# Four weight blocks of the expert stages loaded in pieces of 32, 45, 49 and 2 partitions, two of them late in the stage

## The chip, the cores and the metric

One Trainium2 chip, one core of it. The time is that of one execution on the device, in microseconds (us), the median of the runs shown. The core has five engines with a queue of instructions each: PE (matmul), DVE (vector), ACT (scalar), POOL (GpSimd) and SP (which here only issues DMAs). 16 DMA engines move the data for it.

## What is computed

Two transformer blocks on 256 tokens of 1024 features, one after the other, all in float32. The first block has two layers. Each layer ends in an expert stage (`peer_ffn`): for each token, 8 heads score two sets of 128 keys and choose 16 experts each out of 16384; of every chosen expert one row `u` and one row `v` of 1024 features are read:

```
q = (ht @ w_query).reshape(T, Hh, 2, PEER_HALF)
scores = einsum('thpd,hpkd->thpk', q, sub_keys)
...
u = expert_u[idx]
a = gelu(einsum('tkd,td->tk', u, xb)) * g
return einsum('tk,tkd->td', a, expert_v[idx])
```

So each layer reads 256 x 128 expert rows of 8 KB (u and v together), 256 MB (of 1024 x 1024 bytes). After layer 0's expert stage comes a gated MLP (`sgu`, whose first weight column is `("sgu_v", 6)`); after layer 1's comes the second block, whose mixer starts with the weight column `("w_in", 2)`.

## The kernel before

**Blocks.** Every weight matrix is stored in blocks of 128 partitions x 2048 float32 (1 MB, one row of 8 KB per partition). `blocks` lists them in the order of use. SP loads block i into the buffer `raws[raw_at[i]]` (4 in `ring`, and 2 early ones for each layer's query matrix). Before it is used, a block is split in two: ACT writes the rounded high part to `ring_high` (`highs`, line 2071), DVE the rest in place to `ring_low` (`lows`, line 1241). PE then multiplies in three products (lines 648 and 696).

**The expert stage** (`peer` on each engine). Tokens are on the partitions, 128 at a time, so one layer has 2 x 128 = 256 steps `s`. Step s is one gather by POOL (`gathers`, line 551): row `p_idx[:, s]` of `peer_uv` for each of the 128 partitions, 128 rows of 8 KB, 1 MB. It goes to one of 8 slots (`uv`, 6 in the arena, `uv_high`, 2 in `ring_high`; one of them opens at s = 40, `OPEN_AT`). Then DVE takes the dot product with u (line 1655, semaphore `dot_ready`), ACT makes gelu x gate and a diagonal matrix from it (lines 2258, 2262, 2266), and PE multiplies that matrix with v and adds up in PSUM (line 973, semaphore `uv_used`, which frees the slot: POOL's next gather into it waits for that).

Between the steps stands other work, at fixed s: PE computes the last query columns and scores up to s = 36 (`between`); DVE chooses the experts of the next heads (`choose`); the query blocks and the first blocks of the next matrix are split. At s = 40 POOL first waits for the last scores (line 919), since the slot that opens lies over tiles that they are computed from.

**The order around the change.** SP's queue is one loop over the blocks. For block i it waits until the block that was in the buffer has been used (`wait_block_free`), then issues one DMA. In layer 0 the blocks `first+4` to `first+7` (`first` is the first query block) are followed by `first+8` and `first+9`, the two blocks of `("sgu_v", 6)`; the block after them waits until all 256 dots are done (`behind_rows`). In layer 1 the query blocks are followed by eight blocks of `mem_kv`, and then by the two of `("w_in", 2)`. In both layers the blocks in question are first multiplied at s = 216 and 224 (`TILE_AT`). In layer 0 they are split together, by ACT at s = 40 and DVE at s = 42:

```
sp.dma_start(raws[raw_at[i]], blocks[i]).then_inc(w_in[raw_at[i]], 16)      # SP, line 512
highs(first + 9)        # ACT, s == 40
lows(first + 9)         # DVE, s == 42
```

In layer 1 the same calls split the first two `mem_kv` blocks; the two `w_in` blocks are split there by ACT at s = 154 and 170 and by DVE at s = 157 and 173. ACT waits for `16 * raw_count[i]` on the buffer's semaphore before it splits a block; `raw_count` counts the DMAs into that buffer so far.

## Time and profile before

| | us |
|---|---|
| median of 3 runs | 2271.21 (2267.56 to 2271.28) |
| the profiled execution | 2266.26 |
| its span, first to last instruction | 2264.5 |
| PE, DVE, ACT, POOL busy | 1979.4, 1561.4, 1023.1, 619.8 |

The profiled execution spends 1.8 us outside its span. In the profile, "DMA share" is the mean busy share of the 16 DMA engines (records overlap by a per cent, so that 1.01 is all of them busy), "GB/s" what they moved, and "idle" the time that an engine stood still before an instruction, with the one that ended it. "PEclk" is the TensorE clock granted, as a share of full speed; it is 0.98 over the span. The first expert stage runs from about 278 to 943 us, the second from about 1200 to 1882 us.

### The profile page before, as it was taken

What the parts mean: (1) busy time and instruction counts of PE and PEld (TensorE: products, weight loads), DVE (VectorE), ACT (ScalarE), POOL (GpSimd) and SP (SyncE); (2) the same over time, 40 slices, a digit from 0 to 9 for tenths busy, and PEclk for the clock granted to TensorE, in tenths of its full rate; (3) what the DMA queues carried; (4) which work ended last, traced back from release to release, by engine and by line L of the source; (5) the groups of instructions that cost most, each with busy time, mean ns of one, the idle gap of its engine ahead of it and who ended that gap; (6) DMA issues with size and microseconds to landing.
All of it is one profiled execution on the core that took longest, in us unless ns stands there. A gap on an engine that the chain in (4) does not pass through costs nothing. (4 is left out here: it accounts for less than half of the span.)

```text
span 2264.5 us, 23976 instructions
## 1 busy us (share of the span) xinstructions
PE 1979.4 (87%) x8056; PEld 1237.2 (55%) x8056; DVE 1561.4 (69%) x2947; ACT 1023.1 (45%) x2157; POOL 619.8 (27%) x559
## 2 busy tenths in 40 slices
PE   5999899778777888899989988888888879899998
PEld 4986766223222333379866534334333326878987
DVE  6977787766667776578877777667777755565654
ACT  4344345444444444445444554344464434544443
POOL 0000044543434434100003544443444440310000
PEclk9999999999999999999999999999999999999999
DMA  8886699999999999886669999999999995333553
GB/s 325 295 335 204 247 403 402 417 421 421 421 421 421 422 421 421 337 326 241 220 248 369 407 421 421 420 422 421 421 410 422 421 421 211 118 134 135 179 193 132
DMA packets 112396, 761.24 MB, mean 336 GB/s; under 512 B 12832, under 2 KB 13600, under 8 KB 26128
## 3 DMA queue, kind: packets, MB, share of 16 engines
q0 software_dynamic: 76480, 548.94, 58.6%
q1 hardware_dynamic: 34832, 207.74, 24.8%
q10 hardware_dynamic: 960, 3.01, 0.4%
q8 instruction: 64, 1.05, 0.2%
q14 instruction: 60, 0.49, 0.1%
HBM read 758.60 MB, written 1.05 MB: 335 GB/s over the span
## 5 line engine op out<-in xcount | busy, mean ns | idle before, releaser
L973 PE MATMUL pair<-uv,p_diag 128*128 128x512 f32 x1536 | 755.1, 626 | 175.0 <-ACT p_diag L2266 171.7
L1655 DVE CUSTOM_DVE_ANT_0 uv<-uv,p_h 128x1024 f32<-128x1024 f32 x384 | 469.8, 1224 | 300.7 <-DMA uv<-in_peer_uv,p_idx 299.4
L551 POOL DMA_INDIRECT uv<-in_peer_uv,p_idx x384 | 433.8, 1130 | 684.6 <-PE pair L973 552.7
L973 PEld LDWEIGHTS pair<-uv,p_diag 128*128 128x128 f32 x1536 | 277.4, 194 | 618.3 <-ACT p_diag L2266 363.3
L1241 DVE TENSOR_TENSOR ring_low<-ring,ring_high 128x2048 fp32r<-128x2048 f32 x144 | 328.9, 2297 | 115.4 <-ACT ring_high L2071 114.2
L2258 ACT ACTIVATE p_act<-p_dot 128x1 f32<-128x1 f32 x512 | 103.4, 202 | 625.4 <-DVE p_dot L1655 623.5
L2071 ACT ACTIVATE ring_high<-ring 128x2048 fp32r<-128x2048 f32 x144 | 271.5, 1908 | 176.6 <-DMA ring<-in_ret_w_in 49.5
L696 PE MATMUL pair<-hT_high,ring_high 128*128 128x256 f32 x960 | 286.4, 298 | 1.3 <-ACT b_cgT L2158 1.2
L973 PE MATMUL pair<-uv_high,p_diag 128*128 128x512 f32 x512 | 248.3, 617 | 36.1 <-ACT p_diag L2266 36.1
L696 PE MATMUL pair<-hT_low,ring_high 128*128 128x256 f32 x960 | 271.8, 283 | 0.0
L696 PE MATMUL pair<-hT_high,ring_low 128*128 128x256 f32 x896 | 253.8, 283 | 0.0
L2266 ACT ACTIVATE p_diag<-ident,p_w 128x128 f32<-128x128 f32 x512 | 205.6, 402 | 17.2
L1655 DVE CUSTOM_DVE_ANT_0 uv_high<-uv_high,p_h 128x1024 f32<-128x1024 f32 x128 | 156.6, 1223 | 80.9 <-DMA uv_high<-in_peer_uv,p_idx 79.4
L973 PEld LDWEIGHTS pair<-uv_high,p_diag 128*128 128x128 f32 x512 | 93.3, 194 | 182.1 <-ACT p_diag L2266 94.8
L696 PEld LDWEIGHTS pair<-hT_high,ring_high 128*128 128x128 f32 x960 | 184.4, 192 | 11.3 <-issue 9.6
L696 PEld LDWEIGHTS pair<-hT_low,ring_high 128*128 128x128 f32 x960 | 184.4, 192 | 7.8 <-issue 7.7
L551 POOL DMA_INDIRECT uv_high<-in_peer_uv,p_idx x128 | 144.9, 1132 | 141.5 <-PE pair L973 108.2
L2262 ACT ACTIVATE p_w<-p_act,p_gate 128x1 f32<-128x1 f32 x512 | 150.7, 294 | 49.2 <-ACT p_act L2258 0.8
L696 PEld LDWEIGHTS pair<-hT_high,ring_low 128*128 128x128 f32 x896 | 172.0, 192 | 0.0
L648 PE MATMUL pair<-ring_high,hT_high 128*128 128x512 f32 x240 | 97.7, 407 | 5.2 <-DVE ring_low L1241 3.7
L648 PE MATMUL pair<-ring_high,hT_low 128*128 128x512 f32 x240 | 94.1, 392 | 0.0
L648 PE MATMUL pair<-ring_low,hT_high 128*128 128x512 f32 x240 | 94.1, 392 | 0.0
(395 smaller groups left out, 2432.8 us busy)
## 6 DMA issues: line engine op xcount, KB each, us to landing
ada<-in_ada_w SPq DMA_DIRECT2D x50, 512.0 KB, 5.7
ring<-in_ret_w_in SPq DMA_DIRECT2D x24, 1024.0 KB, 6.4
ring<-in_sgu_w_in SPq DMA_DIRECT2D x24, 1024.0 KB, 6.2
ring<-in_w_up SPq DMA_DIRECT2D x16, 1024.0 KB, 4.8
ring<-in_w_down SPq DMA_DIRECT2D x16, 1024.0 KB, 4.7
mod<-in_ada_w SPq DMA_DIRECT2D x30, 512.0 KB, 6.5
ring<-in_peer_w_query SPq DMA_DIRECT2D x12, 1024.0 KB, 7.8
ring<-in_sgu_w_out SPq DMA_DIRECT2D x12, 1024.0 KB, 6.2
```

Of the source, the lines that this page charges most:

```text
L551: nc.gpsimd.indirect_dma_start(uv_rows[SLOT[l][s]].rearrange("p a d -> p (a d)"), None, experts, bass.IndirectOffsetOnAxis(ap=p_idx[:, k:k ...
L648: mm = nc.tensor.matmul(acc[:, t, :], a, b[:, k, :], start=(first and k == 0 and j == 0), stop=(last and k == BK - 1 and j == 2))
L696: mm = nc.tensor.matmul(acc[:, nt // 2, nt % 2 * S:(nt % 2 + 1) * S], a[:, k, n_tile], b[:, kk, :], start=(kk == 0 and nt % 2 == 0 and j = ...
L973: mm = nc.tensor.matmul(acc[:, half, :], p_diag[:, n % DIAGS, :], v[:, half * 512:(half + 1) * 512], start=(k == 0), stop=(k == PICKS - 1))
L1241: did(V.tensor_tensor(raw_lows[raw_at[i]], raws[raw_at[i]], ring_high[:, high_at[i]].bitcast(F32), ALU.subtract), w_low, i + 1)
L1655: V.tensor_tensor_reduce(out=u, in0=u, in1=p_h[:, s // PICKS, :], scale=1.0, scalar=0.0, op0=ALU.mult, op1=ALU.add, accum_out=p_dot[:, n % ...
L2071: did(A.activation(ring_high[:, high_at[i]], raws[raw_at[i]], ACT.Copy), w_high, i + 1)
L2258: did(A.activation(p_act[:, d:d + 1], p_dot[:, d:d + 1], ACT.Gelu_apprx_tanh))
L2262: did(A.activation(p_w[:, d:d + 1], p_act[:, d:d + 1], ACT.Copy, scale=p_gate[:, s % PICKS:s % PICKS + 1]))
L2266: did(A.activation(p_diag[:, n % DIAGS, :], ident[:], ACT.Copy, scale=p_w[:, d:d + 1]), diag_ready, n + 1)
```

## The change

Four blocks, the two of `("sgu_v", 6)` and the two of `("w_in", 2)`, are each loaded by four DMAs in place of one: partitions 0 to 31, 32 to 76, 77 to 125 and 126 to 127, that is 32, 45, 49 and 2. The bytes are the same, and ACT waits for all four. The two blocks of layer 0 are also issued later: SP waits for dot 140 and dot 156 before them. They are split one at a time, by ACT at s = 150 and 166 and by DVE at s = 152 and 168. In layer 1 neither the issue nor the split is moved.

```
+LATE_LOAD = (140, 156)
+LATE_SPLIT = (150, 166)
+ROW_GROUPS = ((0, 32), (32, 77), (77, 126), (126, 128))
...
-    raw_count = [sum(raw_at[j] == raw_at[i] for j in range(i + 1)) for i in range(limit)]
+    uneven = [first_block_of[("sgu_v", 6)], first_block_of[("sgu_v", 6)] + 1, first_block_of[("w_in", 2)], first_block_of[("w_in", 2)] + 1]
+    loads_of = [ROW_GROUPS if i in uneven else ((0, P),) for i in range(limit)]
+    raw_count = [sum(len(loads_of[j]) for j in range(i + 1) if raw_at[j] == raw_at[i]) for i in range(limit)]
...
-                sp.dma_start(raws[raw_at[i]], blocks[i]).then_inc(w_in[raw_at[i]], 16)
+                if i in uneven[0:2]:
+                    sp.wait_ge(dot_ready, LATE_LOAD[uneven.index(i)])
+                for lo, hi in loads_of[i]:
+                    sp.dma_start(raws[raw_at[i]][lo:hi], blocks[i][lo:hi]).then_inc(w_in[raw_at[i]], 16)
...
-                        if s == 42:
+                        if l == 1 and s == 42:
                             lows(first + 9)
+                        if l == 0 and s - 2 in LATE_SPLIT:
+                            lows(first + 8 + LATE_SPLIT.index(s - 2))
...
-                            highs(first + 9)
+                            if l == 1:
+                                highs(first + 9)
+                        if l == 0 and s in LATE_SPLIT:
+                            highs(first + 8 + LATE_SPLIT.index(s))
```

SP's queue from the last query block to the first blocks after the stage of layer 0, with what each row waits for. Before:

```order
L512 DMA ring<-in_peer_w_query 128x2048 [waits sum_ready]
L512 DMA ring<-in_sgu_w_in 128x2048 [waits w_used]
L512 DMA ring<-in_sgu_w_in 128x2048 [waits sum_ready]
L512 DMA ring<-in_sgu_w_in 128x2048 [waits dot_ready,w_used]
L512 DMA ring<-in_sgu_w_in 128x2048 [waits sum_ready]
```

and now:

```order
L520 DMA ring<-in_peer_w_query 128x2048 [waits sum_ready]
L520 DMA ring<-in_sgu_w_in 32x2048 [waits dot_ready,w_used]
L520 DMA ring<-in_sgu_w_in 45x2048
L520 DMA ring<-in_sgu_w_in 49x2048
L520 DMA ring<-in_sgu_w_in 2x2048
L520 DMA ring<-in_sgu_w_in 32x2048 [waits dot_ready,sum_ready]
L520 DMA ring<-in_sgu_w_in 45x2048
L520 DMA ring<-in_sgu_w_in 49x2048
L520 DMA ring<-in_sgu_w_in 2x2048
L520 DMA ring<-in_sgu_w_in 128x2048 [waits dot_ready,w_used]
L520 DMA ring<-in_sgu_w_in 128x2048 [waits sum_ready]
```

Two DMAs have become eight, and both groups now also wait for `dot_ready`. The next block behind them waited for `dot_ready` already, so nothing else in SP's queue is held up.

DVE's queue around s = 42 of layer 0 (the rows with `p_dot` are the dot products; the row with x2 splits both blocks). Before:

```order
L1655 ISA uv_high_99,p_dot<-uv_high_99,p_h 128x1024
L1655 ISA p_dot 128x1
L1548 MAX_INDEX p_pos<-p_top,p_s 128x8 x2
L1241 TENSOR_TENSOR ring_low<-ring,ring_high 128x2048 x2
L1655 ISA uv_92,p_dot<-uv_92,p_h 128x1024
L1655 ISA p_dot 128x1
```

and now, first there and then at s = 152:

```order
L1663 ISA uv_high_99,p_dot<-uv_high_99,p_h 128x1024
L1663 ISA p_dot 128x1
L1556 MAX_INDEX p_pos<-p_top,p_s 128x8 x2
L1663 ISA uv_92,p_dot<-uv_92,p_h 128x1024
L1663 ISA p_dot 128x1
...
L1598 TENSOR_SCALAR p_ef<-p_i 128x16
L1600 TENSOR_TENSOR p_idx<-p_ef,p_i 128x16
L1249 TENSOR_TENSOR ring_low<-ring,ring_high 128x2048
L1663 ISA uv_high_98,p_dot<-uv_high_98,p_h 128x1024
```

One split stands now between two dots where two stood before, 110 steps later; the second follows 16 steps behind it.

## Rows read from the trace of the kernel before

**Rows 1.** The page, its head and the 40 slices of the span.
```profile
span 2264.5 us, 23976 instructions
...
DMA  8886699999999999886669999999999995333553
GB/s 325 295 335 204 247 403 402 417 421 421 421 421 421 422 421 421 337 326 241 220 248 369 407 421 421 420 422 421 421 410 422 421 421 211 118 134 135 179 193 132
```

**Rows 2.** The costliest groups, both expert stages: busy, mean ns, idle before, releaser.
```profile
L973 PE MATMUL pair<-uv,p_diag 128*128 128x512 f32 x1536 | 755.1, 626 | 175.0 <-ACT p_diag L2266 171.7
L1655 DVE CUSTOM_DVE_ANT_0 uv<-uv,p_h 128x1024 f32<-128x1024 f32 x384 | 469.8, 1224 | 300.7 <-DMA uv<-in_peer_uv,p_idx 299.4
L551 POOL DMA_INDIRECT uv<-in_peer_uv,p_idx x384 | 433.8, 1130 | 684.6 <-PE pair L973 552.7
```

**Rows 3.** Timeline of POOL at the end of stage 0: start, duration, idle before.
```profile
895.27 0.93 POOL L551 DMA_INDIRECT uv<-in_peer_uv,p_idx  x1 [1.54 <-PE pair L973]
...
925.06 0.93 POOL L551 DMA_INDIRECT uv<-in_peer_uv,p_idx  x1 [1.54 <-PE pair L973]
```

**Rows 4.** Stage 0's end by windows: length, engines' busy, PEclk, DMA share, GB/s.
```profile
core 0: us, PE busy (x) PEld busy (x) DVE busy (x) ACT busy (x) POOL busy (x), PEclk, DMA share, GB/s
...
925.00:932.00 7.00, 5.70 (x12) 2.03 (x12) 3.70 (x6) 2.27 (x9) 0.93 (x1) 1.00 1.01 421
932.00:933.00 1.00, 0.50 (x2) 0.25 (x2) 0.13 (x1) 0.67 (x2) 0.00 (x0) 1.00 0.79 328
933.00:934.00 1.00, 1.00 (x3) 0.43 (x3) 1.00 (x1) 0.00 (x0) 0.00 (x0) 1.00 0.45 188
934.00:936.00 2.00, 1.52 (x4) 0.49 (x3) 0.80 (x3) 0.90 (x3) 0.00 (x0) 1.00 0.12 49
936.00:938.00 2.00, 1.55 (x4) 0.49 (x3) 0.77 (x3) 0.90 (x3) 0.00 (x0) 1.00 0.14 57
938.00:940.00 2.00, 1.64 (x4) 0.38 (x2) 1.01 (x2) 0.83 (x3) 0.00 (x0) 1.00 0.05 20
```

**Rows 5.** Timeline of DVE at stage 0's end: the last dots, the first exit step.
```profile
937.77 1.23 DVE L1655 CUSTOM_DVE_ANT_0 uv<-uv,p_h 128x1024 f32<-128x1024 f32 x1 [1.23 <-DMA uv<-in_peer_uv,p_idx]
...
940.23 1.23 DVE L1655 CUSTOM_DVE_ANT_0 uv<-uv,p_h 128x1024 f32<-128x1024 f32 x1 [1.22 <-DMA uv<-in_peer_uv,p_idx]
...
943.85 0.69 DVE L1755 TENSOR_TENSOR p_tmp<-pair,mod 128x512 f32<-128x512 f32 x1 [2.39 <-PE pair L973]
```

**Rows 6.** Stage 1's end by the same windows.
```profile
1873.00:1874.00 1.00, 0.67 (x2) 0.00 (x0) 0.07 (x2) 0.77 (x3) 0.00 (x0) 1.00 0.98 410
1874.00:1875.00 1.00, 0.82 (x2) 0.49 (x3) 0.67 (x1) 0.13 (x1) 0.00 (x0) 1.00 0.40 164
1875.00:1876.00 1.00, 1.00 (x3) 0.19 (x1) 0.57 (x2) 0.30 (x2) 0.00 (x0) 1.00 0.20 82
1876.00:1878.00 2.00, 1.49 (x4) 0.68 (x4) 1.21 (x2) 0.59 (x2) 0.00 (x0) 1.00 0.11 45
1878.00:1879.00 1.00, 0.66 (x2) 0.00 (x0) 0.02 (x2) 0.82 (x3) 0.00 (x0) 1.00 0.04 16
```

**Rows 7.** Timeline of SP's DMA queue: the layer 0 loads, the layer 1 loads; then `ring`'s own view, 280 to 420.
```profile
287.75 6.08 SPq L512 DMA_DIRECT2D ring<-in_sgu_w_in  x2
...
1541.80 356.87 SPq L512 DMA_DIRECT2D ring<-in_w_in  x6
...
L512 SPq DMA_DIRECT2D ring<-in_sgu_w_in x2: 327/328/328, 287.7 to 293.5; - x2
...
DMA to landing us min/median/max: 9.3/9.4/9.6
```

**Rows 8.** Stage 0's first half by windows.
```profile
281.00:303.00 22.00, 18.36 (x118) 14.91 (x118) 15.42 (x57) 8.98 (x16) 6.34 (x6) 0.92 1.01 422
303.00:313.00 10.00, 10.00 (x51) 6.70 (x50) 8.17 (x23) 7.28 (x17) 5.52 (x4) 1.00 1.01 420
313.00:331.00 18.00, 16.77 (x72) 10.14 (x71) 17.09 (x41) 9.93 (x25) 11.20 (x7) 1.00 0.97 381
331.00:357.00 26.00, 26.00 (x117) 16.43 (x117) 19.71 (x44) 15.44 (x38) 14.69 (x12) 1.00 1.00 411
357.00:389.00 32.00, 32.00 (x125) 18.60 (x125) 21.89 (x58) 13.71 (x42) 12.40 (x12) 1.00 1.01 419
389.00:394.00 5.00, 5.00 (x25) 3.09 (x24) 3.38 (x11) 4.24 (x10) 2.39 (x3) 1.00 0.75 286
```

**Rows 9.** Timeline of POOL at s = 40: the wait for the last scores.
```profile
391.00 0.57 POOL L538 DMA_DIRECT2D s_wsT<-in_ws_turned  x1 [6.03 <-PE small L919]
```

**Rows 10.** Timelines of ACT and DVE: the two blocks split at s = 40 and 42.
```profile
401.37 3.71 ACT L2071 ACTIVATE ring_high<-ring 128x2048 fp32r<-128x2048 f32 x2
...
406.61 4.47 DVE L1241 TENSOR_TENSOR ring_low<-ring,ring_high 128x2048 fp32r<-128x2048 f32 x2
```

**Rows 11.** The DMA queue's issues: KB each, us from issue to landing.
```profile
ring<-in_sgu_w_in SPq DMA_DIRECT2D x24, 1024.0 KB, 6.2
```

## The prediction

> **What bounds the kernel now.** I read the head of the page first. Over both expert stages the 16 DMA engines are busy and move 421 GB/s [rows 1]; together the stages are some 1350 of the 2264.5 us. The costliest groups say the same from the engines' side: each dot product waits for its gathered rows (299.4 us of idle time), ACT's and PE's idle time follows from that, and POOL waits for PE, which frees the slots [rows 2]. At the end of stage 0, 13 gathers are issued from 895.27 to 925.06, so one every 29.79 / 12 = 2.48 us [rows 3]. That is 1 MB at 421 GB/s. A weight block is also 1 MB [rows 11], so loading one inside the stage takes 2.49 us of all 16 engines. In rows: a gather or a block is 128 rows of 8 KB, 8 for each DMA engine, and a row takes one engine 2.49 / 8 = 0.311 us.
>
> Next I read how the stage ends, as that tells whether the 16 engines finish together. They don't. In stage 0 all are busy until 932; from 932 to 934 the share falls from 0.79 to 0.45, and from 934 to 938 it is 0.12 to 0.14, which is 2 of 16; then one is left, into the last us before 940 [rows 4]. All that time dots still start every 2.46 us and wait for a DMA, the last at 940.23 [rows 5]. So the pace at the end is that of two DMA engines that lag. I put the ordinary fourteen at 933.3 (the middle of their fall), the laggards at 938.2 and 939.8. The busy time left after 932 is 0.79 + 0.45 + 0.24 + 0.28 + 0.10 = 1.86 us of all 16: spread evenly, the work would end at 933.9, **6 us sooner**. Stage 1 has the same tail: ordinary ones near 1874.3, laggards at about 1877.6 and 1878.8 [rows 6]. The even end there would be 1873 + (0.98 + 0.40 + 0.20 + 0.22 + 0.04) = 1874.8, **4 us sooner**. These 10 us are the most that dealing the bytes out differently can bring.
>
> Last I read stage 0's first half, since two loads leave it. The blocks are issued at 287.75 and 293.5, while the DMA share is 1.01 [rows 7, 8]. But PE is as full there: 10.00 of 10, 16.77 of 18, 26.00 of 26 and 32.00 of 32 us from 303 to 389, and the next gate, POOL's wait for the last scores, ends at 391.00 by PE [rows 8, 9]. DMA and PE bind together until s = 40.
>
> **Part 1, the loads and splits of layer 0 move from the first gathers and s = 40 to s = 140 and 150.** Removed early: 2 x 2.49 = 5.0 us of DMA time. What the gate at 391 gains is between 0 (PE is full) and 5.0 (DMA alone binds); no row shows the stage with less to load. PE's only slack from 303 to 389 is 1.23 us [rows 8], so the value lies near the low end: I take 0.7. The laggards carry some of the early load past the gate, though: their lag is 6.3 us over 659 us of stage, in proportion 1.1 us by 394, where the share has fallen to 0.75 and so ordinary engines are already idle [rows 8]. I take 1.5 us that they catch up beside the 0.7 (ends 0 and 4.3).
> Added late: the same bytes, in a stretch where every engine is busy to the end, so here they cost in full. Dealt out evenly that is 5.0 us on each engine.
> The splits: 3.71 us of ACT and 4.47 us of DVE stood at s = 40 and 42 [rows 10]; now half of each comes at 150 and again at 166. Both are hidden by the gathers in flight: the last one was issued at 925.06 and used at 940.23, 15 us later [rows 3, 5], six gathers deep, so 2.3 us of delay starves no DMA engine. If that cover were gone, each split would cost up to 2.3 us. A load is issued some 25 us before its split, against 9.4 us from issue to landing of the two loads in question [rows 7]. SP issues six more DMAs per layer, on a queue with nothing else in it.
>
> **Part 2, the pieces.** No row shows how 45 or 49 partitions are dealt out, as all large loads here have 128. I assume whole equal shares over as many of the 16 as divide the count, from the first engine on: 32 = 16 x 2, 45 = 15 x 3, 49 = 7 x 7, 2 = 2 x 1. Then a block gives 13 rows to two engines, 12 to five, 5 to eight and 2 to the last one, where each had 8. For the two blocks of a stage, at 0.311 us a row, that is 8.1, 7.5, 3.1 and 1.2 us in place of 5.0. The ends are an even spread (nothing changes) and shares that put the load on the laggards (a loss). I assume the laggards among the lightly loaded nine, one with 2 rows and one with 5.
> What the rows alone show is that two engines lag. The Trainium skill names a pair: in "DMA: Bandwidth & Descriptors", under "Latency and other measured facts", engines 7 and 15 are usually slower where the descriptors come from software. Under "Why a DMA increments its semaphore by 16 and not by 1" the same page gives the deal assumed above, on the lowest-numbered engines; by it engine 7 gets 5 rows and engine 15 gets 2. By these two rules the sum is the one below.
>
> **The sum.** Stage 0, everything 0.7 sooner after the gate: the laggards end at 939.8 - 0.7 - 1.5 + 1.2 = 938.8 and 938.2 - 0.7 - 1.5 + 3.1 = 939.1, the heavily loaded at 933.3 - 0.7 + 8.1 = **940.7**. The last was at 939.8: +0.9 us. So the lag is filled up, but with work that was free before. Stage 1, where nothing moves and the loads come at 1541.80 and later, in the full stretch [rows 7]: the laggards 1878.8 - 3.7 = 1875.1 and 1877.6 - 1.9 = 1875.7, the heavily loaded 1874.3 + 3.1 = **1877.4**: -1.4 us. Together **-0.5 us**. The profiled execution would go from 2266.3 to 2265.8 us. It stood 4.9 us below the median of the runs, so for the median I say 2271.2 - 0.5 = **2270.7 us**.
>
> **The rivals.**
> *The early DMA time counts* (faster). If the first gathers and not PE set the time to s = 40, the gate gains some 4 us. For it: the share 1.01 from 281 to 313. Against it: PE at 10.00 of 10 and 32.00 of 32. Stage 0 then ends at 933.3 - 4 + 8.1 = 937.4 (-2.4), stage 1 brings -1.4 to, where the heavily loaded ones are the first of the fourteen to finish, -2.6: -3.8 to -5.0 us, about 2266.5.
> *The laggards are among the heavily loaded* (slower). The trace doesn't number its DMA engines. If a laggard gets 13 rows a block, stage 0 ends at 939.8 - 0.7 - 1.5 + 8.1 = 945.7 (+5.9) and stage 1 at 1878.8 + 3.1 = 1881.9 (+3.1): +9.0, 2280 us. It decides as soon as a laggard gets more than 8 rows. For it: the rows leave open which engines lag. Against it: both tails are alike, two laggards of nearly the same size, so the lag seems to belong to a fixed pair, and nine of the 16 are lightly loaded. I choose 0.10, below what a blind draw of the pair would give. What keeps it low is the pair that the Trainium skill names, above.
> *The pieces don't change the deal.* If every engine still gets 8 rows, only the move is left: 939.8 - 0.7 - 1.5 + 5.0 = 942.6, +2.8 us in stage 0 and 0 in stage 1, 2274.0. The trace can't exclude it.
> A rule speaks for this one. In its "Rules for kernel authors" the same page of the Trainium skill advises one transfer of 128 partitions over transfers to disjoint parts, since they serialize on the same engines: by that the pieces bring nothing and the sum is this rival's.
>
> **How the numbers follow.** What a measurement of this kernel can tell from no change is about 0.2%, 4.5 us. The forecast has a chance of 0.55, the first rival 0.25, the second 0.10, the third 0.10. The forecast lies within 4.5 us of no change with nearly all its weight: its own bounds are +3 (no gain at the gate, no catching up) and -3. The first rival I count as faster, though half of it lies at the bound; the second is slower, and of the third 0.03, as the runs scatter by 3.7 us. So faster 0.25, the same 0.62, slower 0.13. The range runs from 2264.0 (the first rival, with a us for the runs' scatter) to 2275.5 (the third rival, with a little more); it leaves out the second rival and the far end of the first.
>
> **What would show it.** In the windows at the end of the stages the tail should be short: the share falls in steps over the last 2 to 3 us, five to seven engines finish last rather than two, and there is no stretch of 4 us at 0.12. The last dot of stage 0 should start at about 941, in stage 1 about 1.4 us sooner counted from that stage's start. At the gate, POOL's wait should end within a us of 391, and the share between 389 and 394 should be lower than 0.75 or fall earlier. The layer 0 loads should be issued near 650 and 690. A tail that is longer than before, with one or two engines, would show the laggards were loaded; a tail as before in stage 1 shows the pieces are dealt evenly; a gate at 387 shows the first rival. The forecast is wrong if the time moves by over 4.5 us.

## The result, and the profile after

Before: 2271.24 us (median of 4 runs, 2267.56 to 2273.85). After: **2299.34 us** (4 runs, 2297.72 to 2302.56). The ratio is 1.014, with a 95% interval of 1.0126 to 1.0155: 1.4% slower. The medians are 28 us apart; 1.4% of 2268 us is 32 us (29 to 35). Forecast were 2270.7 and at most 2275.5 us. The execution that was profiled took 2302.56 us, with a span of 2300.8. It is the slowest of its four, and the profiled one of before (2266.26 us) is faster than the median, so the two traces lie 36 us apart, more than the medians.

The page of the kernel after, its head and the costliest groups, which answer to [rows 1, 2]:

```profile
span 2300.8 us, 23991 instructions
...
DMA  8886699999999999886669999999999996333453
GB/s 322 291 331 213 252 359 407 422 422 421 421 385 362 421 421 421 338 340 232 223 245 373 404 420 421 420 422 382 355 402 423 421 421 231 113 135 131 183 191 137
...
L981 PE MATMUL pair<-uv,p_diag 128*128 128x512 f32 x1536 | 769.1, 636 | 193.5 <-ACT p_diag L2276 190.6
L1663 DVE CUSTOM_DVE_ANT_0 uv<-uv,p_h 128x1024 f32<-128x1024 f32 x384 | 470.4, 1225 | 333.5 <-DMA uv<-in_peer_uv,p_idx 333.1
```

The dots are as long as before (1225 ns) and wait 33 us longer for their rows: 333.1 where 299.4 stood. The GB/s line has two holes that weren't there, 385 and 362 in stage 0, 382 and 355 in stage 1, while the DMA digits above them stay 9. The engines don't stand idle; they are busy and move less. The windows around the two loads of layer 0, and then of layer 1 (length, busy time and count of PE, PEld, DVE, ACT and POOL, PEclk, DMA share, GB/s), put the holes where the loads are:

```profile
640.00:651.00 11.00, 10.00 (x22) 3.89 (x21) 8.08 (x25) 4.04 (x14) 6.66 (x6) 0.97 1.01 422
651.00:667.00 16.00, 9.21 (x16) 2.90 (x14) 4.69 (x14) 2.69 (x9) 3.72 (x5) 0.82 1.01 288
667.00:701.00 34.00, 24.92 (x46) 9.53 (x47) 25.10 (x60) 16.16 (x43) 12.70 (x12) 0.85 1.02 423
701.00:718.00 17.00, 10.35 (x19) 3.61 (x17) 4.51 (x15) 2.69 (x9) 5.63 (x5) 0.87 1.01 282
718.00:724.00 6.00, 3.78 (x4) 1.17 (x4) 5.69 (x7) 0.90 (x3) 0.00 (x0) 0.60 1.02 423
724.00:736.00 12.00, 10.38 (x20) 4.47 (x20) 9.44 (x24) 8.05 (x21) 5.16 (x5) 0.78 0.87 328
```

```profile
1550.00:1562.00 12.00, 12.00 (x40) 7.26 (x39) 9.37 (x27) 5.55 (x14) 3.73 (x3) 1.00 1.02 422
1562.00:1578.00 16.00, 10.28 (x20) 3.85 (x19) 5.75 (x12) 2.80 (x10) 6.56 (x6) 0.89 1.02 281
1578.00:1612.00 34.00, 28.92 (x66) 13.88 (x67) 24.03 (x62) 14.84 (x43) 11.15 (x11) 0.85 1.01 420
1612.00:1630.00 18.00, 11.88 (x28) 4.72 (x26) 7.25 (x16) 4.92 (x13) 7.31 (x7) 1.00 1.02 283
```

Each load is followed by 16 to 18 us at 281 to 288 GB/s, at a DMA share of 1.01 or 1.02. What a window loses is its length times (1 - rate / 421): 5.1, 5.6, 5.3 and 5.9 us, 21.9 in all. After the second load of layer 0 there is a different loss. From 724 to 736 the share itself falls, to 0.87: no gather was issued in time, 12 x (1 - 328/421) = 2.7 us. Stage 1 has a like dip some 50 us after its second load, from 1660 to 1673; here are the dip, and the whole stretch from the first load to its end:

```profile
1660.00:1673.00 13.00, 12.74 (x35) 6.24 (x33) 10.76 (x28) 6.25 (x16) 6.42 (x5) 1.00 0.84 314
1560.00:1673.00 113.00, 90.06 (x202) 40.14 (x200) 68.82 (x168) 44.27 (x119) 42.83 (x38) 0.89 0.99 365
```

The whole stretch loses 113 x (1 - 365/421) = 15.0 us. Stage 1, counted from its first gather to its last dot, took 695.9 us where it had taken 680.7: the 15.2 are all there. Stage 0, counted in the same way, grew by 17.3 us, from 661.8 to 679.2.

How it reaches the other engines shows in DVE's timeline over the first load (start, duration, idle before and its releaser). Dots that came every 2.46 us [rows 5] come 6.8 and 7.7 us apart:

```profile
653.11 1.22 DVE L1663 CUSTOM_DVE_ANT_0 uv<-uv,p_h 128x1024 f32<-128x1024 f32 x1 [0.85 <-DMA uv<-in_peer_uv,p_idx]
...
659.88 1.23 DVE L1663 CUSTOM_DVE_ANT_0 uv<-uv,p_h 128x1024 f32<-128x1024 f32 x1 [5.00 <-DMA uv<-in_peer_uv,p_idx]
...
667.56 1.23 DVE L1663 CUSTOM_DVE_ANT_0 uv<-uv,p_h 128x1024 f32<-128x1024 f32 x1 [6.03 <-DMA uv<-in_peer_uv,p_idx]
```

And POOL, which issues the next gather into a slot that a finished row frees, then waits for PE, so the late rows come back a second time as late gathers:

```profile
657.71 0.94 POOL L559 DMA_INDIRECT uv<-in_peer_uv,p_idx  x1 [1.55 <-PE pair L981]
666.27 0.94 POOL L559 DMA_INDIRECT uv<-in_peer_uv,p_idx  x1 [7.63 <-PE pair L981]
674.23 0.94 POOL L559 DMA_INDIRECT uv<-in_peer_uv,p_idx  x1 [7.02 <-PE pair L981]
```

The single packets of the trace say what the engines do in those 16 us. A packet of 8 KB takes 314 ns elsewhere in the stage, nearly without scatter, whichever queue it is of. While the pieces of a block are in flight, for 13.5 to 14.8 us, 70 to 87% of the packets take 400 to 620 ns and 2 to 5% stay under 330, with a mean of 494 to 520 over the four blocks, **the gathers' packets no less than the load's**. The starts of the load's packets also fit the deal that the prediction assumed: two waves of 16, then 45 in waves that run into each other, then seven waves of 7, some 1 us apart, then 2. Which engine takes which row they don't show, as the trace doesn't number the engines.

The places that the prediction had named, in the order SP's timeline, the gate on POOL and the end of stage 0 (windows, then the last dot), for [rows 7, 9, 4, 5]:

```profile
649.46 51.39 SPq L520 DMA_DIRECT2D ring<-in_sgu_w_in  x8
```

```profile
279.59 1.03 POOL L559 DMA_INDIRECT uv<-in_peer_uv,p_idx  x1 [84.54 <-DVE p_idx L1628]
...
392.20 0.57 POOL L546 DMA_DIRECT2D s_wsT<-in_ws_turned  x1 [6.03 <-PE small L927]
```

```profile
303.00:313.00 10.00, 10.00 (x53) 6.93 (x52) 9.33 (x30) 6.76 (x17) 5.12 (x4) 1.00 0.79 270
...
389.00:394.00 5.00, 4.66 (x24) 2.78 (x22) 2.76 (x8) 4.61 (x10) 1.49 (x2) 1.00 0.90 371
...
951.00:953.00 2.00, 1.79 (x4) 0.68 (x4) 1.23 (x2) 0.43 (x3) 0.00 (x0) 1.00 0.48 201
953.00:957.00 4.00, 3.02 (x7) 1.17 (x7) 1.95 (x3) 1.52 (x5) 0.00 (x0) 1.00 0.14 57
957.00:958.00 1.00, 1.00 (x3) 0.19 (x1) 0.52 (x2) 0.35 (x2) 0.00 (x0) 1.00 0.10 41
```

```profile
958.74 1.23 DVE L1663 CUSTOM_DVE_ANT_0 uv<-uv,p_h 128x1024 f32<-128x1024 f32 x1 [1.22 <-DMA uv<-in_peer_uv,p_idx]
```

From the first gather to the gate it took 392.20 - 279.59 = 112.61 us; before it was 391.00 - 278.40 = 112.60. Nothing was gained there, though the DMA engines moved 270 GB/s from 303 to 313 in place of 420: PE was full then, as before. The share around the gate, forecast below the 0.75 of before, was 0.90. The tail at stage 0's end is as long as it was, two engines for 4 to 5 us; the five to seven engines that were to finish last aren't seen.

### The profile page after: what moved, and what is told of

Its sections match the earlier page's. It is cut to its first block and busy times, and to the rows that moved or that the text cites. A ratio compares the mean times of both kernels' runs of the same rounds, so it can differ in the third digit from the quotient of the medians.

```text
span 2300.8 us, 23991 instructions
## 1 busy us (share of the span) xinstructions
PE 1990.4 (87%) x8056; PEld 1243.0 (54%) x8056; DVE 1563.4 (68%) x2947; ACT 1022.9 (44%) x2157; POOL 616.8 (27%) x559
## 5 line engine op out<-in xcount | busy, mean ns | idle before, releaser
L981 PE MATMUL pair<-uv,p_diag 128*128 128x512 f32 x1536 | 769.1, 636 | 193.5 <-ACT p_diag L2276 190.6
L1663 DVE CUSTOM_DVE_ANT_0 uv<-uv,p_h 128x1024 f32<-128x1024 f32 x384 | 470.4, 1225 | 333.5 <-DMA uv<-in_peer_uv,p_idx 333.1
L981 PEld LDWEIGHTS pair<-uv,p_diag 128*128 128x128 f32 x1536 | 283.1, 198 | 646.0 <-ACT p_diag L2276 382.6
L559 POOL DMA_INDIRECT uv<-in_peer_uv,p_idx x384 | 427.1, 1112 | 719.2 <-PE pair L981 582.7
```

The source lines that it names most:

```text
L559: nc.gpsimd.indirect_dma_start(uv_rows[SLOT[l][s]].rearrange("p a d -> p (a d)"), None, experts, bass.IndirectOffsetOnAxis(ap=p_idx[:, k:k ...
L981: mm = nc.tensor.matmul(acc[:, half, :], p_diag[:, n % DIAGS, :], v[:, half * 512:(half + 1) * 512], start=(k == 0), stop=(k == PICKS - 1))
L1663: V.tensor_tensor_reduce(out=u, in0=u, in1=p_h[:, s // PICKS, :], scale=1.0, scalar=0.0, op0=ALU.mult, op1=ALU.add, accum_out=p_dot[:, n % ...
```

## The experiments

Each change to the time is the ratio less 1, times 2268 us, with its 95% interval; "before" was run beside each batch (medians 2267.9 to 2268.7, 13 to 21 runs a batch). "Only in layer 1" means that the two `w_in` blocks, loaded in the full stretch after 1541, are the only ones touched. All others load as before. Where a stage's own time is given, it is that of the one profiled execution, from the first gather to the last dot; stage 0 takes 660.6 to 662.2 us in the sixteen traces in which nothing in it was changed, so a difference of a us or so in it says nothing.

### Taking the change apart

**late_whole**: the move alone, `ROW_GROUPS` not used.

```diff
-    loads_of = [ROW_GROUPS if i in uneven else ((0, P),) for i in range(limit)]
+    loads_of = [((0, P),) for i in range(limit)]
```

> The changed kernel with its four blocks loaded whole again; only the move of layer 0's two loads and splits to s = 140 to 168 is left. After the change stage 0 (first gather issued to last dot) grew by 17.3 us and stage 1 by 15.3 us; at 651 to 667 and 701 to 718 us, right after the loads of pieces, the DMA share stayed 1.01 while 288 and 282 GB/s were moved in place of 421. Theory 1, the pieces slow all DMA while they are loaded, whenever that is: late_whole costs only the 5.0 us of DMA time that were free before, at most, +2 to +5 us against before, no window under 415 GB/s around the loads. Theory 2, a load that falls into the full stretch costs much more than its bytes: +15 to +20 us, and low GB/s at the same places.

**pieces_early**: the pieces in all four blocks, loads and splits at their old places (the waits and the places of `lows` and `highs` as in the kernel before).

> The kernel before with the four blocks in pieces of 32, 45, 49 and 2 partitions, nothing moved. Theory 1: layer 1's stage as in the changed kernel, +15 us; in layer 0 the slow stretch falls on the time in which PE binds as well as the DMAs, so it costs between 3 and 10 us; in all +18 to +25 us. Theory 2 (the late place is what costs): +15 us or less, all of it in layer 1, and nothing in layer 0.

**pieces_layer1**: the pieces only in layer 1, nothing moved.

```diff
-    uneven = [first_block_of[("sgu_v", 6)], first_block_of[("sgu_v", 6)] + 1, first_block_of[("w_in", 2)], first_block_of[("w_in", 2)] + 1]
+    uneven = [first_block_of[("w_in", 2)], first_block_of[("w_in", 2)] + 1]
```

> Pieces of 32, 45, 49 and 2 for the two w_in blocks of layer 1 alone. Theory 1: stage 0 as before within 2 us, stage 1 +15 us (two stretches of 16 to 18 us at about 280 GB/s), in all +13 to +17 us. If the slow stretches needed something of layer 0's change, it would be under 5 us.

Measured: late_whole 2273.11 us, 1.0016 [1.0007, 1.0026], **+3.6** (1.6 to 5.9). pieces_early 2292.26, 1.0111 [1.0094, 1.0128], **+25** (21 to 29). pieces_layer1 2281.01, 1.0066 [1.005, 1.0083], **+15** (11 to 19). By the traces, stage 0 grew by 4.7, 9.2 and -1.1 us in these three and stage 1 by 1.2, 14.2 and 16.5. So the pieces carry the loss, wherever they are; the move adds a little. In late_whole the window over the first load is as full as ever; in pieces_layer1 the same hole is there (the first fence is late_whole's windows, the second those of pieces_layer1):

```profile
651.00:667.00 16.00, 11.60 (x21) 3.80 (x20) 8.35 (x22) 4.49 (x15) 4.68 (x5) 0.89 1.02 421
```

```profile
1541.00:1558.00 17.00, 12.60 (x26) 4.81 (x24) 7.35 (x17) 4.79 (x11) 5.85 (x6) 0.85 1.02 299
...
1587.00:1610.00 23.00, 17.62 (x52) 9.27 (x50) 11.37 (x31) 7.09 (x19) 11.88 (x9) 1.00 1.01 310
```

### More DMAs, or other partitions? Only in layer 1

**two_64_layer1**

```diff
+ROW_GROUPS = ((0, 64), (64, 128))
```

> The two w_in blocks loaded as halves, partitions 0 to 63 and 64 to 127: each engine's share of a block is even again, and there are two DMAs. Theory U, the uneven shares do it (seven engines have to carry 49 of 128 rows): no slow stretch, 421 GB/s throughout, 0 us. Theory P, a load that goes to a part of the partitions crowds a part of the ways into SBUF, which the gathers need too: slow stretches again, and +5 to +15 us. Theory N, the number of DMAs: a third of the cost or less, +2 to +5 us.

**two_strided_layer1**: the even partitions, then the odd ones.

```diff
+                        sp.dma_start(raws[raw_at[i]][lo::2], blocks[i][lo::2]).then_inc(w_in[raw_at[i]], 16)
```

> The two w_in blocks in halves again, but the even and the odd partitions in place of 0 to 63 and 64 to 127. Two contiguous halves cost 4.2 thousandths (9.5 us), with stretches of 10 us at 280 GB/s. Theory P (a load to one stretch of partitions crowds a part of the ways into SBUF): each half now reaches all of them, so no slow stretch, 415 to 421 GB/s throughout, and 0 to +2 us. Theory N (more DMAs, or 64 partitions in place of 128, are what costs): +9 us as with the contiguous halves.

**four_cols_layer1**: four DMAs of all 128 partitions, a quarter of the columns each (a block's row stands in the buffer as four runs of 512).

```diff
+ROW_GROUPS = ((0, 1), (1, 2), (2, 3), (3, 4))
...
+                        sp.dma_start(raws[raw_at[i]][:, lo:hi], blocks[i][:, lo:hi]).then_inc(w_in[raw_at[i]], 16)
```

> The two w_in blocks in four DMAs each, but cut along the row: 128 partitions x 512 floats (2 KB) each. Same number of DMAs as in the change. Theory P: every DMA reaches all partitions, so the stretches stay above 400 GB/s, 0 to +3 us (2 KB packets may be a little dearer). Theory N, the number of DMAs: +13 to +17 us as with the four pieces of the change.

**uneven_strided_layer1**: strided pieces of 45, 49, 16, 15 and 3.

```diff
+ROW_GROUPS = ((0, 90), (1, 99), (90, 122), (99, 128), (122, 128))
...
+                    step = 2 if i in uneven else 1
+                    sp.dma_start(raws[raw_at[i]][lo:hi:step], blocks[i][lo:hi:step]).then_inc(w_in[raw_at[i]], 16)
```

> The two w_in blocks in strided pieces (every second partition) of 45, 49, 16, 15 and 3. By equal whole shares that is nearly the uneven deal of the change: 13 rows for three DMA engines, 12 for four, 5 for eight, 1 for the last. Theory P: the pieces reach all the ways into SBUF, so most of the cost of the change in layer 1 (+15 us) goes; -2 to +4 us. Theory U (the uneven deal itself holds up the gathers): +10 us or more, and slow stretches as in the change. If it is under 0, the uneven deal does relieve the two late engines.

**three_48_layer1**

```diff
+ROW_GROUPS = ((0, 48), (48, 96), (96, 128))
```

> The two w_in blocks in contiguous pieces of 48, 48 and 32 partitions: every one deals evenly over 16 engines (3, 3 and 2 rows). Theory P: each piece crowds a part of the ways, as the halves do; +8 to +15 us, slow stretches near 300 GB/s. Theory U: 0 us, as all shares are even. Theory T, counts that are no power of two are what costs: more than the halves' +9.5 us.

Measured: two_64 2276.81 us, 1.0042 [1.0025, 1.0059], **+9.5** (6 to 13). two_strided 2268.6, 0.9999 [0.999, 1.0009], **0** (-2 to 2). four_cols 2269.68, 1.0001 [0.9991, 1.0011], **0** (-2 to 2). uneven_strided 2283.04, 1.0059 [1.0043, 1.0076], **+13** (10 to 17). three_48 2275.58, 1.0036 [1.0023, 1.0049], **+8** (5 to 11). The same window in two_64 and in two_strided:

```profile
1541.00:1558.00 17.00, 13.32 (x30) 5.74 (x29) 9.26 (x24) 5.51 (x13) 5.61 (x5) 0.90 1.02 334
```

```profile
1541.00:1558.00 17.00, 14.96 (x38) 6.78 (x37) 11.80 (x27) 6.30 (x16) 9.75 (x7) 1.00 1.01 421
```

Same bytes, same number of DMAs, the same 4 rows for each engine and piece; one costs 9.5 us and the other nothing. So it isn't the number of DMAs (theory N), and four_cols, with as many DMAs as the change, says the same. three_48 has even shares and costs 8 us, so the uneven shares (theory U) aren't the whole cause either, and with less than the halves' 9.5 us it gives nothing to theory T. My idea then was theory P, that 64 neighbours crowd half of the ways into the chip's memory. uneven_strided missed that: its pieces reach over most of the partitions and still cost 13 us, its packets being slow as well (348 GB/s in this window).

### On which side, and what is uneven about it

**dst_contig_src_strided** and **dst_strided_src_contig**. In both, the rows of the two blocks land in other partitions than the multiplication needs, so only their time is of use:

```diff
+                        sp.dma_start(raws[raw_at[i]][64 * lo:64 * lo + 64], blocks[i][lo::2]).then_inc(w_in[raw_at[i]], 16)
```

```diff
+                        sp.dma_start(raws[raw_at[i]][lo::2], blocks[i][64 * lo:64 * lo + 64]).then_inc(w_in[raw_at[i]], 16)
```

> The two layer 1 blocks are loaded as two DMAs each: partitions 0 to 63 and 64 to 127 on chip, from the even and from the odd rows of the block in HBM. The rows of these two blocks so land in other partitions than the reference's; the work is otherwise the same. Theory W (the side that is crowded is the write into the chip's partitions): as the two contiguous halves, 7 to 11 us slower than before, 330 to 350 GB/s in 1541 to 1558 us. Theory H (the side is HBM, where 64 neighbouring rows are read at once): within 2 us of before, 421 GB/s.

> The mirror: the even and the odd partitions on chip, from rows 0 to 63 and 64 to 127 of the block in HBM (rows of these two blocks in other partitions than the reference's, the work otherwise the same). Theory W: within 2 us of before, 421 GB/s. Theory H: 7 to 11 us slower, 330 to 350 GB/s in 1541 to 1558 us.

**uneven_63_layer1** (every second partition, as in uneven_strided) and **four_32_layer1**

```diff
+ROW_GROUPS = ((0, 126), (1, 127), (126, 128), (127, 128))
```

```diff
+ROW_GROUPS = ((0, 32), (32, 64), (64, 96), (96, 128))
```

> Pieces spread over all partitions, but uneven over the DMA engines: the 63 even partitions from 0 to 124, the 63 odd ones from 1 to 125, then partitions 126 and 127 alone. 63 = 9 x 7, so nine DMA engines get 14 rows of a block (one of them 16), seven get none. Theory U (an uneven deal costs by itself, as gathers wait for the engines that are loaded): 6 us or more slower than before, with a stretch of less than 400 GB/s after each pair of loads, but packets of 0.31 us. Theory E (only a crowded part of the partitions costs): 421 GB/s during the loads, and at the end of the stage at most what the nine have more, 2 x 6 x 0.311 = 3.7 us; since the lagging two are last before, 0 to 3.7 us in all.

> Four pieces of 32 neighbouring partitions, two rows for each of the 16 DMA engines in each piece, so the deal is even. Theory U (the uneven deal makes the difference between 8 to 9.5 us for contiguous halves or thirds and 15 us for 32, 45, 49, 2): 8 to 10 us slower than before. Theory S (the smaller the part of the partitions that a piece covers, the more it crowds): 13 us or more slower, below 320 GB/s in 1541 to 1558 us.

Measured: neighbouring partitions from strided HBM rows 2277.52 us, 1.004 [1.0026, 1.0054], **+9** (6 to 12); strided partitions from neighbouring rows 2269.25, 1.0003 [0.9993, 1.0013], **+1** (-2 to 3). Their rows, in this order:

```profile
1541.00:1558.00 17.00, 13.44 (x31) 5.91 (x29) 8.62 (x24) 5.40 (x13) 5.24 (x5) 0.90 1.02 310
```

```profile
1541.00:1558.00 17.00, 13.83 (x36) 6.28 (x35) 11.72 (x30) 6.71 (x18) 6.83 (x6) 1.00 1.01 420
```

What counts is the partitions that are written, not the rows that are read (theory W; its 330 to 350 GB/s for the first came out as 310).

uneven_63 2280.72, 1.0057 [1.004, 1.0074], **+13** (9 to 17); four_32 2275.87, 1.0046 [1.0029, 1.0063], **+10** (7 to 14). Theory S (13 us or more, below 320 GB/s; it was 328) falls, and so does E. U's number is met, but not as it said: the packets of uneven_63 aren't 314 ns, their mean is 450 to 479, and for longer. Its pieces are in flight for 13.5 to 14.4 us, those of two_64 and four_32 for 8.3 to 9.4, at 275 to 294 and 244 to 259 GB/s meanwhile. uneven_63 also speaks against P in every form: each piece of 63 reaches the same partitions as the halves of two_strided but one, and those cost nothing. The row of uneven_63, which is to be read beside the 334 above (the rest of its slow stretch lies behind 1558):

```profile
1541.00:1558.00 17.00, 14.71 (x43) 7.56 (x41) 10.08 (x27) 6.29 (x16) 6.01 (x7) 1.00 1.02 353
1558.00:1587.00 29.00, 20.14 (x37) 7.22 (x38) 16.78 (x41) 11.77 (x33) 8.72 (x9) 0.88 1.01 397
```

So **how slow** differs little between the slow kernels (450 to 580 ns a packet), and **how long** goes roughly by the rows of the engine that has most: 8 rows last 7.6 to 10.5 us, 9 rows 10.3 to 12.4, 13 and 16 rows alike 13.1 to 15.1. At a packet of 0.5 us, and with gather rows in turn between the load's, a row takes about 1 us, as the waves of 7 in the change show.

### Whose partitions are they?

**shift_112_layer1**, **rot_120_layer1**, **step_15_layer1** and **step_16_layer1**, one line each (first, last, step):

```diff
+ROW_GROUPS = ((16, 128, 1), (0, 16, 1))
+ROW_GROUPS = ((8, 128, 1), (0, 8, 1))
+ROW_GROUPS = tuple((j, 120, 8) for j in range(8)) + ((120, 128, 1),)
+ROW_GROUPS = tuple((j, 128, 8) for j in range(8))
```

> Two pieces: partitions 16 to 127 (112 = 16 x 7, seven neighbouring rows for each DMA engine) and 0 to 15 (one row each): every engine has 8 rows, and the first piece covers seven eighths of the partitions, but the engine that writes 0 to 7 in a whole load now writes 16 to 22, and so on. Theory O (an engine that writes partitions which belong to another engine in a whole load and in the gathers slows both; all engines are slow until the pieces are through): 6 to 10 us slower than before, below 370 GB/s in 1541 to 1558 us. Theory C (a piece has to cover all the partitions): 0 to 2 us slower, over 400 GB/s. Theory U (the shares have to be even): 0.

> Partitions 8 to 127 (120 = 15 x 8) and 0 to 7 (8 x 1): fifteen engines write eight rows each, but in each case the eight of the next engine; then eight engines write one row. Shares 9, 8 and, for one engine, 0. Theory O: 7 to 11 us slower than before, below 370 GB/s in 1541 to 1558 us. Theory C: 0 to 2 us. Theory U: as step_15_layer1, whatever that is, since the shares are the same.

> Eight pieces of the partitions j, j + 8, ... j + 112 (15 rows, one for each of fifteen engines, in the engine's own eight), and partitions 120 to 127 last (8 x 1): the same shares as in rot_120_layer1, in nine DMAs, but seven eighths and more of the rows are written by their own engine. Theory O: 0 to 2 us slower, over 400 GB/s in 1541 to 1558 us. Theory U: as slow as rot_120_layer1.

> Eight pieces of the partitions j, j + 8, ... j + 120: 16 rows, one for each engine, in its own eight; even shares, eight DMAs for a block. Theories O, C and U: within 1.5 us of before, 421 GB/s. If it is slow, the number of rows in a DMA counts by itself.

Measured: shift_112 2274.24 us, 1.003 [1.0018, 1.0041], **+7** (4 to 9), as O said: even shares and seven eighths of the partitions don't help, which ends C and U as whole explanations. rot_120 2277.14, 1.0036 [1.0021, 1.0051], **+8**; step_15 2276.38, 1.0038 [1.0024, 1.0052], **+9**, where O had 0 to 2 and only U's wording fits, as slow as rot_120. But step_16 2275.13, 1.0033 [1.002, 1.0046], **+7**, with even shares, which no theory had. The rows of shift_112 and of step_16:

```profile
1541.00:1558.00 17.00, 12.31 (x28) 5.20 (x28) 10.46 (x24) 5.60 (x14) 6.81 (x6) 0.96 1.01 347
```

```profile
1541.00:1558.00 17.00, 12.49 (x28) 5.09 (x27) 9.15 (x22) 5.52 (x14) 7.98 (x6) 0.98 1.02 325
```

My picture of an engine's eight neighbouring partitions was the wrong one. The Trainium skill has another, in "SBUF — State Buffer", section "Door 1: The DMA port swizzle (why `[64,N]` ≈ `[32,N]`)": there are 16 ports for DMA, and a port serves a group of four partitions and the group 32 above it; neighbouring groups lie on eight different ports, and partitions 64 to 127 on the other eight. If each engine has one port that it writes in a whole load, and a row is "foreign" when another engine writes it, a stride of eight, which meets only every second group, is foreign too. That is theory G below; a piece of 32 rows with a step of four can follow the pattern.

**step_4_layer1**, and **after_step_4**, the whole change with these pieces in all four blocks:

```diff
-ROW_GROUPS = ((0, 32), (32, 77), (77, 126), (126, 128))
+ROW_GROUPS = tuple((j, 128, 4) for j in range(4))
...
-                for lo, hi in loads_of[i]:
-                    sp.dma_start(raws[raw_at[i]][lo:hi], blocks[i][lo:hi]).then_inc(w_in[raw_at[i]], 16)
+                for lo, hi, step in loads_of[i]:
+                    sp.dma_start(raws[raw_at[i]][lo:hi:step], blocks[i][lo:hi:step]).then_inc(w_in[raw_at[i]], 16)
```

> Four pieces of the partitions j, j + 4, ... j + 124, 32 rows each, two for each DMA engine. Theory G (in a whole load and in the gathers an engine writes a group of four neighbouring partitions and the group 32 above it, eight engines for partitions 0 to 63 and eight for 64 to 127, and any other writer there slows both; 32 rows are dealt in the same pattern, one row in place of four): every row goes to its own engine, so within 1.5 us of before and 421 GB/s in 1541 to 1558 us. It also makes the pieces of step_16_layer1 foreign: a stride of eight gives only every second group. Theory N (a DMA of 16 or 32 rows slows the traffic by itself): 6 to 9 us slower, as four_32_layer1 and step_16_layer1, 320 to 350 GB/s. If the engines took neighbouring rows, two each, they would write two groups each and the result would lie near step_16_layer1 too.

> The whole change, but with the four blocks loaded in pieces of every fourth partition in place of 32, 45, 49 and 2 neighbours; the loads and splits of layer 0 late, as in the change. Theory G: only the move is left, 2 to 6 us slower than before (late_whole: 3.6), 421 GB/s in 651 to 667 us. Theory N: 17 to 22 us slower, below 350 GB/s there.

Measured: step_4 2268.32 us, 1.0007 [0.9997, 1.0016], **+2** by the ratio (-1 to 4) and 0.3 by the medians; after_step_4 2274.11, 1.0025 [1.0016, 1.0035], **+6** (4 to 8), where the change itself has +32 (29 to 35) by the same measure. The rows (step_4 over the first load of layer 1, then after_step_4 over those of layer 0):

```profile
1541.00:1558.00 17.00, 15.31 (x40) 7.11 (x39) 11.48 (x25) 6.69 (x17) 8.12 (x7) 1.00 1.02 421
```

```profile
651.00:667.00 16.00, 10.05 (x21) 3.52 (x22) 8.27 (x21) 4.49 (x15) 5.84 (x6) 1.00 1.01 419
...
701.00:718.00 17.00, 10.10 (x16) 3.89 (x16) 13.97 (x30) 5.42 (x19) 4.83 (x4) 0.80 1.01 422
```

Four pieces of 32 rows, two rows for each engine and piece: as neighbours +10 us, as every fourth partition nothing that can be measured. The row of the neighbours (four_32):

```profile
1541.00:1558.00 17.00, 11.91 (x32) 5.47 (x30) 9.01 (x21) 5.30 (x13) 7.20 (x6) 0.99 1.01 328
```

N falls, and G's numbers came in. The kernels of this study stand to it as follows:

| load of the two layer 1 blocks | does each engine keep to its port, by G | busiest engine, rows | us against before | stage 1 in the trace, us |
|---|---|---|---|---|
| one DMA of 128; 4 of 128, columns | yes | 8 | 0 | 680.7; 683.1 |
| 64 even, 64 odd | yes | 8 | 0 | 681.1 |
| 4 x every 4th | yes | 8 | +2 (-1 to 4) | 681.2 |
| 8 x every 8th | no | 8 | +7 | 689.2 |
| 112 + 16 | no | 8 | +7 | 688.5 |
| 48, 48, 32 | no | 8 | +8 | 690.2 |
| 64 + 64 neighbours | no | 8 | +9.5 | 690.6 |
| 4 x 32 neighbours | no | 8 | +10 | 690.1 |
| 120 + 8 | no | 9 | +8 | 692.1 |
| 8 x 15 every 8th, 8 | no | 9 | +9 | 692.2 |
| 63 even, 63 odd, 1, 1 | no | 16 | +13 | 694.5 |
| 45, 49, 16, 15, 3, strided | no | 13 | +13 | 693.5 |
| 32, 45, 49, 2 (the change) | no | 13 | +15 | 697.2 |

The "yes" of the pieces assumes that a piece of n rows is dealt n/32 rows at a time around eight engines, its first half first, then the other half around the other eight. The "no" needs no such order. With equal shares over the engines of the prediction's deal, and one port for each engine, counting the rows that lie on each port leaves at least 14 of the 128 rows (120 + 8) to 78 (the change) with an engine that isn't the port's own. That count is an estimate from the page's ports, and the cost doesn't go by it: 14 rows cost as much as 64 (8 x every 8th). after_step_4, with the same layer 1 load as step_4, took 684.6 us in stage 1; its 4 us over before aren't at the loads, and even so it lies below every "no".

**What stays open.** That the loss comes with the partitions which a piece writes, and not with the number of DMAs, the HBM side or uneven shares alone, is shown by pairs of runs. That the cause is an engine writing another's port is inferred: the trace numbers neither DMA engines nor ports, so G is supported only by which loads are slow, and it was put together when all the other kernels were known and then met by the last two; that the gathers write in the same pattern is inferred from the whole loads beside them being free. No run loads pieces of this kind without gathers beside them.

## Why the prediction was wrong, point by point

- **What bounds the kernel** was right: both stages are DMA bound and what DMA time was lost in them was paid. It is why the error was so large: 15.0 us lost in the windows of stage 1 are the 15.2 us by which it grew, and in stage 0 13.4 lost there and 4.7 for the move, 18.1, stand beside 17.3.
- **The step that failed is in part 2**: "for the two blocks of a stage, at 0.311 us a row, that is 8.1, 7.5, 3.1 and 1.2 us in place of 5.0". The deal fits the packets. The price of a row was wrong: the 0.311 us come from rows where each engine writes what it writes in a whole load, and I carried it over to pieces where it doesn't. Rows took near 0.5 us, the gathers' rows beside them as well, and for as long as the engine with 13 rows a block had some. Slow stretches and dips cost 15 us in stage 1 and 13.4 in stage 0, where the prediction had the pieces bring 1.4 us in stage 1 and 1.9 in stage 0 (+0.9 in place of the +2.8 of the move alone). It also put nothing for what a load does to the gathers beside it. The ends that I kept for this term, an even spread and shares on the laggards, both took the duration of a packet as given. No row showed a load of less than 128 partitions, and the prediction says so for the deal, but draws no bound from it for the speed.
- **The shift of the shares**, the gain that the pieces were made for, can't be seen. The tail of stage 0 should have shrunk from 6 us to 2 or 3 and is as long as before. Why, no run shows.
- **The rule that was cited** for rival 3, from "DMA: Bandwidth & Descriptors", section "Rules for kernel authors", speaks against the pieces, and against those of the change it was right to. It is written of two halves of the partitions, which serialize; that reason gives the rival's +2.8 us. For neighbouring halves the trace shows worse than that: 64 + 64 neighbours cost 9.5 us. 64 even + 64 odd, disjoint as well, cost nothing. I looked for the rule that sets the number of engines and not for the one that says which partitions an engine writes without meeting another.
- **Part 1, the move.** Forecast as a rival's sum, +2.8; measured alone, +3.6 (1.6 to 5.9). In late_whole the last dot starts 944.94 - 278.46 = 666.5 us after the first gather, before 940.23 - 278.40 = 661.8: +4.7. So if the late load was paid in full, 5.0, the early relief brought about 0.3 (give or take the us or so by which the traces scatter), not 0.7 + 1.5 = 2.2. The gate stood still (112.66 against 112.60; the 114.22 of after_step_4 has its like in the 114.25 of step_4, where stage 0 is as before), as the low end of 0 had it; the laggards' catching up by 1.5, an estimate in proportion, didn't come. Their tail there is as long as ever: in 942 to 943 of late_whole the DMA share is still 0.16.
- **The first rival** (early DMA time counts) is refuted by the same gate. In the kernel after, the DMA engines had less to do early (270 GB/s from 303 to 313) and PE, at 10.00 of 10, took the same time.
- **The second rival** (laggards among the heavily loaded): stage 1's tail, from the fall of the share to the last DMA, went from about 4.5 to 3.5 us (0.30, 0.17, 0.06 from 1909 to 1913), and in stage 0 it is as long as before. The tails didn't grow, as they would with a laggard heavily loaded, but which engines lag isn't settled by it: pieces_layer1, with the same pieces, has a tail of stage 1 as long as before, and over the traces with even shares it runs from 3 to 6 us.
- **The splits** were hidden, as forecast: after_step_4 has all of layer 0's late, and 416 to 425 GB/s in the windows from 640 to 760.
- **The loads** were issued at 649.46 and some 50 us on, forecast near 650 and 690. In late_whole, without the slow stretch between them, the second came at 693.0.
- **Slips in its sums**, which change nothing above: the laggards' lag of 6.3 us is 6.5 and 4.9 by its own ends, and the first rival with a us of scatter gives 2265.2, not the 2264.0 at which the range starts.

The sum, by the parts that were measured alone: the move 3.6, pieces in layer 1 15, pieces in layer 0 about 10 (25 for all four blocks less 15), together about 28.6 us. The change has 32 (29 to 35) by the ratio and 28 by the medians. The 10 is that of pieces at the early place; at the late one the traces give 17.3 - 4.7 = 12.6 us.

## What to carry to other kernels

Beside a stream that fills the DMA engines, the price of a load is more than its bytes: before you cut one, ask which partitions each piece writes and, if theory G holds, whether a DMA engine then writes where another one does. A split by columns, in even and odd partitions or in every fourth of them kept the traffic at 412 to 422 GB/s here; a split into ranges of neighbours, in every eighth partition, or with counts such as 63, 45 and 49, brought it to 230 to 294 GB/s until the engine with the most rows was through. And a DMA share of 1.01 says only that the engines are busy: read it beside the GB/s, and when an operation comes in a shape that no row of the trace shows, its speed is an unknown with bounds of its own, not only its count.

## What the runs showed of the hardware that I had not expected

- A load in pieces of one of these ten shapes (foreign ones, by theory G) slows all DMA traffic of the core, not itself alone: packets of 8 KB go from 314 ns to means between 450 and 580 on both queues, and 421 GB/s to between 230 and 294, while it is in flight. The Trainium skill has a sentence that fits, in "DMA: Bandwidth & Descriptors", section "Back-pressure in remote DMA": stalled writes stall the source engine's other queues too. It is said there of transfers between cores; here the trace shows slow gathers beside slow loads in one core, without showing where a write was held.
- The side is the write into the chip's memory. Halves read from HBM as neighbours but written to strided partitions cost 1 us (-2 to 3), the other way round 9 (6 to 12).
- After 16 us of slow traffic comes a second loss: some 6 us (stage 0) and 30 us (stage 1) after the second load's slow stretch the DMA share falls to 0.87 and 0.84 for 12 to 13 us. Between 708.09 and 724.22 POOL issued only one gather, and PE, busy for 10.35 of 17 us and then 3.78 of 6, had its granted clock at 0.87 and then 0.60 of the full 2.4 GHz in those windows. DVE also stood in the way there: from 719.31 to 723.25 it did other work before it took a dot (5.69 us busy of the 6 from 718 to 724). In the dip of stage 1 the clock was 1.00 and PE busy for 12.74 of 13 us, after 10.00 of 10 at 0.83, so the lowered clock and DVE's other work aren't in both dips alike. Which of them keeps the slots longer wasn't tried.
